# Products with zero-one matrices in fp32r, with a high and a low part

## The reference, cut to what matters

```python
cum = jnp.cumsum(log_f, axis=1).transpose(0, 2, 1)
...
logits = logits + cum[:, :, q0:kl, None] - cum[:, :, None, :kl]
...
p = jax.nn.softmax(jnp.where(mask, logits, NEG_INF), axis=-1)
```

```python
decay_in = jnp.exp(segsum(a))      # segsum[i, j] = sum of a[j+1..i] for i >= j, else -inf
cb = jnp.einsum('bclgn,bcsgn->bgcls', Cc, Bc)
y_diag = jnp.einsum('bgcls,bgrcls,bcsgrp->bclgrp', cb, decay_in, x_dt)
```

## Time and profile before

| | us |
|---|---|
| median of 3 runs (1515.44 to 1515.95) | 1515.65 |
| the profiled execution | 1515.26 |
| its span | 1513.5 |
| TensorE busy | 1435.5 |
| VectorE busy | 1060.0 |
| ScalarE busy | 757.6 |
| GpSimd busy | 70.2 |

### The profile page before, as it was taken

The page is one execution under the profiler, slowest core; times in us unless marked ns, Lnnn a source line. Parts: engine busy times, 40 slices in busy tenths (PEclk is TensorE's granted clock), DMA queues, the critical chain, the costliest instruction groups (busy, mean ns, idle before and its releaser), DMA issues.

```text
span 1513.5 us, 26922 instructions
## 1 busy us (share of the span) xinstructions
PE 1435.5 (95%) x9273; PEld 1293.6 (85%) x9273; DVE 1060.0 (70%) x1981; ACT 757.6 (50%) x1211; POOL 70.2 (5%) x87
## 2 busy tenths in 40 slices
PE   7889889999899997989989999999999999999997
PEld 7867769899798886889979999999999999988886
DVE  6897665555668577569997999555555555567775
ACT  6644654444556533454544555444444444444453
POOL 0200100000000621000000000000000000000000
PEclk9999999999999999999999999999999999999999
DMA  7442325565344522454546888755757566577753
GB/s 280 139 130 96 126 84 188 186 192 183 112 144 161 169 82 70 153 181 154 167 152 185 256 257 259 226 189 184 249 183 245 182 220 210 190 239 249 249 194 140
DMA packets 103208, 274.54 MB, mean 181 GB/s; under 512 B 8160, under 2 KB 41056, under 8 KB 102640
## 3 DMA queue, kind: packets, MB, share of 16 engines
q1 hardware_dynamic: 64832, 237.11, 48.4%
q10 hardware_dynamic: 38032, 34.63, 6.8%
q0 software_dynamic: 288, 2.10, 0.4%
HBM read 254.93 MB, written 18.87 MB: 181 GB/s over the span
## 4 chain that ended last, share of the span: by engine, by line
PE 80%; DVE 15%; ACT 2%; issue 2%; POOL 0%; DMA 0%; POOLq 0%; ACTq 0%; DVEq 0%; SPq 0%
PE Y L1803 43%; PE AO L1803 34%; DVE wl L950 4%; DVE CV L1034 2%; PE M L1803 2%; ACT wh L471 1%; DVE eqs L1558 1%; DVE I L1478 1%; DVE SCO L1494 1%; DVE I L1492 1%; DVE PU L1533 0%; DVE V L1500 0%; DVE V L1486 0%; DVE eqs L1572 0%; DVE xn L973 0%
## 5 line engine op out<-in xcount | busy, mean ns | idle before, releaser
L950 DVE TENSOR_TENSOR wl<-raw,wh 128x1024 fp32r<-128x1024 f32 x440 | 541.6, 1234 | 278.2 <-ACT wh L471 277.4
L471 ACT CAST wh<-raw 128x1024 fp32r<-128x1024 f32 x440 | 460.0, 1048 | 186.7 <-PE AO L1803 92.3
L1803 PE MATMUL AO<-xh,wh 128*128 128x256 f32 (+1 forms) x1776 | 511.0, 288 | 8.6 <-DVE wl L950 7.3
L1803 PE MATMUL AO<-xh,wl 128*128 128x256 f32 (+1 forms) x1776 | 503.4, 283 | 0.0
L1803 PE MATMUL AO<-xl,wh 128*128 128x256 f32 (+1 forms) x1776 | 503.4, 283 | 0.0
L1803 PEld LDWEIGHTS AO<-xh,wh 128*128 128x128 f32 x1776 | 338.5, 191 | 16.3 <-DVE wl L950 9.0
L1803 PEld LDWEIGHTS AO<-xl,wh 128*128 128x128 f32 x1776 | 337.8, 190 | 4.6 <-issue 0.2
L1803 PEld LDWEIGHTS AO<-xh,wl 128*128 128x128 f32 x1776 | 338.7, 191 | 0.0
L1803 PE MATMUL Y<-wh,peer_ah 128*128 128x512 f32 x512 | 200.7, 392 | 2.1 <-DVE peer_al L1620 2.1
L1803 PE MATMUL Y<-wh,peer_al 128*128 128x512 f32 x512 | 200.3, 391 | 0.0
L1803 PE MATMUL Y<-wl,peer_ah 128*128 128x512 f32 x512 | 199.1, 389 | 0.0
(11 more groups left out here) (305 smaller groups left out, 1672.2 us busy)
## 6 DMA issues: line engine op xcount, KB each, us to landing
raw<-in_stream SPq DMA_DIRECT2D x440, 512.0 KB, 3.4
gate_spill<-gstage ACTq DMA_DIRECT2D x32, 512.0 KB, 5.2
gates<-gate_spill ACTq DMA_DIRECT2D x6, 2048.0 KB, 14.9
gates<-gate_spill ACTq DMA_DIRECT2D x8, 512.0 KB, 7.2
rowg<-in_post SPq DMA_DIRECT2D x3, 512.0 KB, 4.4
X<-in_x SPq DMA_DIRECT2D x2, 512.0 KB, 4.8
memx<-in_mem SPq DMA_DIRECT2D x1, 1024.0 KB, 8.1
keys<-in_keys POOLq DMA_DIRECT2D x1, 1024.0 KB, 6.7
```

Source lines behind the costliest of these rows:

```text
L471: nc.scalar.copy(wh[:, s, :], raw[:, s, :]).then_inc(split_hi, 1)
L950: nc.vector.tensor_tensor(wl[:, s, :], raw[:, s, :], wh[:, s, :].bitcast(F32), ALU.subtract)\
L1803: return nc.tensor.matmul(o, a, b, start=start, stop=stop)
```

## The change

The operands of the products with zero-one matrices become fp32r. As fp32r holds fewer bits than float32, the other operand is split: a high part (the value rounded to fp32r) and a low part (the rest), each multiplied by the same zero-one matrix into the same accumulation.

- VectorE: two more steps after the forget logarithms (a copy to fp32r and a subtraction, tile logs) and two more after dt_a (tile da), each waiting for the one before.
- GpSimd: DEC is made twice (DEC and DECL), six products in place of three, the second three behind an added wait for norm_turned 4, as DECL lies where xn was; AU is made twice per k (AU and AUL), two products in place of one. A wait for da_split is added ahead of the scan's work.
- TensorE: logits and seg use fp32r products, twice as many for the decays and the segment sums; the mask product stays single, with 2 to the 100 in place of 1e30, a number that fp32r holds.
- The waits for DEC count to 6, those for AU to 2k + 2.

The products of queries and keys, of MM and XDT, of the states, of ac (line 2091 and on) and the turns stay plain float32.

```diff
@@ -36,6 +36,7 @@
 NEG = -1e30
+MASKED = 2.0 ** 100
 SLOTS = 4
@@ -150,11 +151,13 @@
         xl = sb("xl", [P, KT, TM], F32R)
-        ident = sb("ident", [P, P])
+        ident_r = sb("ident", [P, P], F32R)
+        ident = ident_r[:, :].bitcast(F32)
         masks_at = (nc.sbuf_base + 31) // 32 * 32
-        upper = sb("upper", [P, P])
-        later = sb("later", [P, P])
-        ones = sb("ones", [P, P])
+        upper_r = sb("upper", [P, P], F32R)
+        later_r = sb("later", [P, P], F32R)
+        ones_r = sb("ones", [P, P], F32R)
+        upper, later, ones = (t[:, :].bitcast(F32) for t in (upper_r, later_r, ones_r))
         neg_half = sb("neg_half", [P, 1])
@@ -173,7 +176,7 @@
         rowg = at("rowg", [P, 3, D], 8768)
-        mask = at("mask", [P, P], 21056)
+        mask = at("mask", [P, P], 21056, F32R)
         memx = at("memx", [P, TT, D], 22080)
@@ -186,7 +189,8 @@
         MV = at("MV", [P, TT, 512], 100384)
-        DEC = at("DEC", [P, FOX_H, 3, P], 104480)
+        DEC = (at("DEC", [P, FOX_H, 3, P], 104480, F32R), at("DECL", [P, FOX_H, 3, P], 63520, F32R))
+        logs = at("logs", [P, 2, 16], 59424 + 64, F32R)
         att_p = at("att_p", [P, 2, 512], 116768)
@@ -215,7 +219,8 @@
         CBM = at("CBM", [P, 4, P], 98336)
-        AU = at("AU", [P, 2, 3, P], 124192)
+        AU = (at("AU", [P, 2, 3, P], 124192, F32R), at("AUL", [P, 2, 3, P], 0, F32R, base=choice_at))
+        da = at("da", [P, 2, 2 * SSD_H], 78048, F32R)
         EE = at("EE", [P, 2, 3, P], 127264)
@@ -294,6 +299,7 @@
         cb_prod, cb_mask, ac_prod, ac_exp = sem("cb_prod"), sem("cb_mask"), sem("ac_prod"), sem("ac_exp")
+        da_split = sem("da_split")
         xdd_w, xdd_done, xdt_done, xd_done = sem("xdd_w"), sem("xdd_done"), sem("xdt_done"), sem("xd_done")
@@ -594,7 +600,7 @@
                     values_high(s - 2)
-                    act.wait_ge(dec_done, 3)
+                    act.wait_ge(dec_done, 6)
                     act.wait_ge(ln_xc, 1)
@@ -1069,6 +1075,12 @@
                     nc.vector.tensor_tensor(zf, z8, zf, ALU.subtract).then_inc(logf, 1)
+                    dve.wait_ge(logf, 1)
+                    z16 = SQ[:, 0, 0:16]
+                    nc.vector.tensor_copy(logs[:, 0, :], z16).then_inc(logf, 1)
+                    dve.wait_ge(logf, 2)
+                    nc.vector.tensor_tensor(logs[:, 1, :], z16, logs[:, 0, :].bitcast(F32), ALU.subtract)\
+                        .then_inc(logf, 1)
@@ -1257,6 +1269,11 @@
                     .then_inc(dt_a, 1)
+            dve.wait_ge(dt_a, 2)
+            nc.vector.tensor_copy(da[:, 0, :], dtz[:, 3, 24:72]).then_inc(da_split, 1)
+            dve.wait_ge(da_split, 1)
+            nc.vector.tensor_tensor(da[:, 1, :], dtz[:, 3, 24:72], da[:, 0, :].bitcast(F32), ALU.subtract)\
+                .then_inc(da_split, 1)
@@ -1673,21 +1690,21 @@
             nc.gpsimd.memset(ident[:, :], 0.0).then_inc(consts, 1)
-            nc.gpsimd.memset(mask[:, :], 0.0).then_inc(consts, 1)
+            nc.gpsimd.memset(mask[:, :].bitcast(F32), 0.0).then_inc(consts, 1)
             nc.gpsimd.memset(neg_half[:, :], -0.5).then_inc(consts, 1)
...
             pool.wait_ge(consts, 5)
-            nc.gpsimd.affine_select(out=ident[:, :], in_=ident[:, :], pattern=[[-1, P]], compare_op=ALU.not_equal,
+            nc.gpsimd.affine_select(out=ident_r[:, :], in_=ident[:, :], pattern=[[-1, P]], compare_op=ALU.not_equal,
                                     fill=1.0, base=0, channel_multiplier=1).then_inc(consts, 1)
-            nc.gpsimd.affine_select(out=upper[:, :], in_=ones[:, :], pattern=[[1, P]], compare_op=ALU.is_ge,
+            nc.gpsimd.affine_select(out=upper_r[:, :], in_=ones[:, :], pattern=[[1, P]], compare_op=ALU.is_ge,
                                     fill=0.0, base=0, channel_multiplier=-1).then_inc(consts, 1)
-            nc.gpsimd.affine_select(out=later[:, :], in_=ones[:, :], pattern=[[-1, P]], compare_op=ALU.is_gt,
+            nc.gpsimd.affine_select(out=later_r[:, :], in_=ones[:, :], pattern=[[-1, P]], compare_op=ALU.is_gt,
                                     fill=0.0, base=0, channel_multiplier=1).then_inc(consts, 1)
-            nc.gpsimd.affine_select(out=mask[:, :], in_=mask[:, :], pattern=[[-1, P]], compare_op=ALU.is_ge,
-                                    fill=-NEG, base=0, channel_multiplier=1).then_inc(consts, 1)
+            nc.gpsimd.affine_select(out=mask[:, :], in_=mask[:, :].bitcast(F32), pattern=[[-1, P]], compare_op=ALU.is_ge,
+                                    fill=MASKED, base=0, channel_multiplier=1).then_inc(consts, 1)
@@ -1716,11 +1733,14 @@
             pool.wait_ge(consts, 9)
-            pool.wait_ge(logf, 1)
-            zf = SQ[:, 0, 0:16].rearrange("p (j h) -> p j h", j=TT)
-            for n, (j, m) in enumerate(((0, later), (1, ones), (1, later))):
-                nc.gpsimd.tensor_tensor(DEC[:, :, n, :], zf[:, j, :][:, :, None].to_broadcast([P, FOX_H, P]),
-                                        m[:, None, :].to_broadcast([P, FOX_H, P]), ALU.mult).then_inc(dec_done, 1)
+            for part in range(2):
+                pool.wait_ge(logf, 2 + part)
+                if part:
+                    pool.wait_ge(norm_turned, 4)
+                z = logs[:, part, :].bitcast(F32).rearrange("p (j h) -> p j h", j=TT)
+                for n, (j, m) in enumerate(((0, later), (1, ones), (1, later))):
+                    nc.gpsimd.tensor_tensor(DEC[part][:, :, n, :], z[:, j, :][:, :, None].to_broadcast([P, FOX_H, P]),
+                                            m[:, None, :].to_broadcast([P, FOX_H, P]), ALU.mult).then_inc(dec_done, 1)
             for p in range(3):
@@ -1741,9 +1761,10 @@
                     pool.wait_ge(seg_prod, k - 1)
-                a = dtz[:, 3, 24 * (c + 1) + 3 * s:24 * (c + 1) + 3 * s + 3]
-                nc.gpsimd.tensor_tensor(AU[:, k % 2, :, :], a[:, :, None].to_broadcast([P, 3, P]),
-                                        upper[:, None, :].to_broadcast([P, 3, P]), ALU.mult).then_inc(au_done, 1)
+                for part in range(2):
+                    a = da[:, part, 24 * c + 3 * s:24 * c + 3 * s + 3].bitcast(F32)
+                    nc.gpsimd.tensor_tensor(AU[part][:, k % 2, :, :], a[:, :, None].to_broadcast([P, 3, P]),
+                                            upper[:, None, :].to_broadcast([P, 3, P]), ALU.mult).then_inc(au_done, 1)
@@ -1763,6 +1784,7 @@
             pool.wait_ge(xdd_w, 2)
+            pool.wait_ge(da_split, 2)
             pool.wait_ge(tr_out, 3)
@@ -1958,13 +1980,14 @@
                 if kind != "mem":
-                    d = DEC[:, :, :, :].rearrange("p (a e) n k -> p e a n k", e=2)[:, e, 2 * m:2 * m + n, :, :]
-                    if kind == "first":
-                        mm(o, upper[:, :], d[:, :, 0, :], True, False)
-                    else:
-                        mm(o, upper[:, :], d[:, :, 1:3, :].rearrange("p a n k -> p a (n k)"), True, False)
-                        mm(o[:, :, 0:P], ones[:, :], d[:, :, 0, :], False, False)
-                    mm(o[:, :, w - P:], ident[:, :], mask[:, None, :].to_broadcast([P, n, P]), False, False)
+                    for part in range(2):
+                        d = DEC[part][:, :, :, :].rearrange("p (a e) n k -> p e a n k", e=2)[:, e, 2 * m:2 * m + n, :, :]
+                        if kind == "first":
+                            mm(o, upper_r[:, :], d[:, :, 0, :], part == 0, False)
+                        else:
+                            mm(o, upper_r[:, :], d[:, :, 1:3, :].rearrange("p a n k -> p a (n k)"), part == 0, False)
+                            mm(o[:, :, 0:P], ones_r[:, :], d[:, :, 0, :], False, False)
+                    mm(o[:, :, w - P:], ident_r[:, :], mask[:, None, :].to_broadcast([P, n, P]), False, False)
                 for i, (h, j, w) in enumerate(members(g)):
@@ -1996,7 +2019,7 @@
             pe.wait_ge(norm_lo, 4)
-            pe.wait_ge(dec_done, 3)
+            pe.wait_ge(dec_done, 6)
             pe.wait_ge(a_free, A_BASE["qk"] + 8)
@@ -2169,11 +2192,13 @@
             def seg(k):
-                pe.wait_ge(au_done, k + 1)
+                pe.wait_ge(au_done, 2 * k + 2)
                 if k:
                     pe.wait_ge(seg_exp, k)
-                mm(AO[:, 0, 0:3 * P], later[:, :], AU[:, k % 2, :, :].rearrange("p a b -> p (a b)"),
-                   True, True).then_inc(seg_prod, 1)
+                for part in range(2):
+                    ins = mm(AO[:, 0, 0:3 * P], later_r[:, :], AU[part][:, k % 2, :, :].rearrange("p a b -> p (a b)"),
+                             part == 0, part == 1)
+                ins.then_inc(seg_prod, 1)
```

## The result

The changed kernel took **1521.82 us**, the median of 5 runs (1517.49 to 1522.54), against 1515.65 for the kernel before (1514.17 to 1515.95, 5 runs): a ratio of 1.0036, 95% interval 1.002 to 1.0051. Two later sets of runs gave +3.1 and +5.2 us. The profiled run is the fastest of the first five, 1517.49 us with a span of 1515.8, so its trace understates the difference.

What follows compares the result with a forecast made beforehand. TensorE carries 80% of the span, but VectorE bounds the forgetting attention. Terms 2.9 + 0.4 + 1.4 + 1.8 = +6.5 us on the profiled 1515.26, with 0.4 for the median, gave 1522.2 us; range 1515.0 to 1527.5.

Steps and rivals of the forecast that it cites:

- Three more DEC products: Forgetting attention: GpSimd's three added products hold up VectorE, +4.0 us, bounds 2.0 and 7.4.
- VectorE's waits for groups 4 and 5: Attention logits: faster TensorE removes VectorE's waits of 0.56 and 0.95 us, −1.5 us.
- Two steps after the forget logarithms: Attention: VectorE's added copy and subtraction, 0.2 us each, +0.4 us, bounds 0.1 and 0.8.
- Attention in sum: Forgetting attention, its three terms together: 4.0 + 0.4 − 1.5 = +2.9 us.
- Two steps after dt_a: Ahead of the xbc conv: VectorE's copy and subtraction, +0.4 us (0.1 to 0.8), all on the chain.
- First chunk: Scan: six AU pairs cost VectorE 3.3 us, less idle time and slack, +1.4 us, bounds −2.1 and +3.5.
- Second chunk: Scan: added AU products delay MM steps, two segment sums give back 0.6, +1.8 us, bounds −1.0 and +4.0.
- stages that I took as untouched: The rest of the kernel: fp32r constants, MASKED and moved tiles change no count or size, nothing added.
- the products win: Rival: GpSimd's added work costs nothing and TensorE's savings arrive, −3.8 us, 1511.8 us; chance 0.10.
- Half of it: Rival: attention costs as forecast but the scan absorbs its pairs (−1.0), +2.3 us, 1518.0 us; chance 0.17.
- It doesn't do what it says: Rival: fp32r products run at the plain pitch, so TensorE pays twice, about 1531 us; chance 0.03.
- The clock: Rival: longer pauses bring two or three more TensorE clock dips, adding 2.6 to 3.9 us, 1525.5 us; chance 0.15.

Runs made afterwards that it cites:

- e4: Kernel before with GpSimd making the three DEC products a second time into an unread tile, matmuls plain float32: 1519.9 us, ratio 1.0027.
- e3: Changed kernel with GpSimd making only the high DEC and AU, each multiplied twice by TensorE: 1512.22 us, ratio 0.9982 to the kernel before.
- e11: The changed kernel run a third time, nothing else altered: 1520.52 us against 1515.31 for the kernel before.
- e2: Kernel before with the scan part of the change alone (with the two steps after dt_a), attention as before: 1514.4 us, ratio 0.9993.
- e10: The scan part of the change alone on the kernel before, run again: 1514.76 us against 1515.31.
- e7: Whole change, but ScalarE makes both parts of DEC and the low part of AU: 1511.44 us, ratio 0.9974 to the kernel before.
- e12: Kernel before with only the copy and subtraction after dt_a added, results unread: 1511.56 us, ratio 0.9972.

## Why the prediction was right, and where it was not

The time was right to 0.4 us (1522.2 against 1521.8), but three sets of runs spread over 3 us, and the spans of the three traces are only 2.3, 3.1 and 4.4 us longer than before, as stages outside of the sum gave time back. So close a hit is luck; what held is the direction, and above all the cost of the DEC products. By the steps of the sum:

- **Three more DEC products, +4.0**: 3.94 in the rows, 3.95 in e4. The ml steps spared 0.9 us of the fourth product, as worked out. The upper bound for the fp32r type wasn't needed.
- **VectorE's waits for groups 4 and 5, −1.5**: both gone, and e3 has −1.3 for the stage, with the two small steps in it. One group's zero-one products took 0.99 us, not 0.82, and had taken 1.82, not 1.72; counted from the turns ahead of them the group saved 0.90, as I had it.
- **Two steps after the forget logarithms, +0.4**: starts at 62.83, 63.03, 63.24. Attention in sum +2.7, predicted +2.9.
- **Two steps after dt_a, +0.4**: +0.5 between the last dtz step and XDM, in each of the eight traces that have them. But I took all of it to reach the end. It doesn't: the next stage gives back 1.4, by the dip at 490 to 496 us. This step of the sum failed in its sign: with that dip it is −0.9, and the kernel with nothing but these steps is 3.75 us faster, the part beyond −0.9 unexplained.
- **First chunk, +1.4**: +0.4, the term mis-sized. I took 0.55 us for each pair, 3.3 in all; VectorE's busy time grew by 2.35 in the whole chunk, as the second products partly met steps that read PSUM (the ST step at 559.27 took 0.56) and VectorE's idle time. And "its shorter segment sums come to nothing" was too strict: with its waits between sums (1.65 at k = 2, 0.69 at k = 4), TensorE's 2.07 us less of work counted against 2.47 of waiting. MM for k = 4 came later than TensorE was ready, and so did k = 2, which I hadn't named; at k = 7, the other that I named, it was late by 0.1 us only.
- **Second chunk, +1.8**: +2.2, with the same clock (0.89) before and after. Late are a split (1.84 at 571.49), a YO sum (1.31) and an SP step (1.06), as the lock has it.

The terms sum to +5.8 us where I had +6.5. The stages that I took as untouched moved as well: by +0.6 to −1.3 between the conv and dt_a, by −1.4 behind XDM, and by −2.3 or +0.5 at the end, depending on the run. The third trace of the change (e11) shows the slow end of this: windows of the first trace, then of e11:

```profile
780.00:790.00 10.00, 7.70 (x60) 7.30 (x61) 9.93 (x15) 5.40 (x8) 0.00 (x0) 1.00 0.34 112
810.00:820.00 10.00, 7.45 (x64) 7.28 (x63) 8.96 (x21) 4.10 (x7) 0.00 (x0) 1.00 0.38 129
```

```profile
780.00:790.00 10.00, 7.57 (x51) 7.49 (x51) 9.93 (x13) 4.03 (x6) 0.00 (x0) 0.83 0.33 105
810.00:820.00 10.00, 7.44 (x53) 7.27 (x52) 8.38 (x21) 4.10 (x7) 0.00 (x0) 0.85 0.34 119
```

The same kernel, two dips more, 2.8 us more from the last gate to the end. The Trainium skill, "TensorE: Matmul & The Clock Gate", section "Part 1: The HAM clock gate (the "warmup" mystery)", says that the point at which the clock first rises can differ between runs of one kernel. These two traces show such a difference in the middle of a kernel: 1.00 in one and 0.83 in the other at 780 to 790 us.

Of the rivals, "the products win" fell with e4. "Half of it" had the scan at −1.0 and fell with its +0.4 and +2.1 in the change, e2 and e10, though the +3.1 of the second set of runs alone would not have ruled it out. "It doesn't do what it says" fell with the pitches: 0.12 us for 256 columns, 0.18 for 384. "The clock" was half right. It expected longer pauses to bring dips at the scan; there are as many as before. New ones came in the attention (0.76 at 98 to 112 us, before 1.00), where VectorE sets the end and the stage came out as summed. What it missed is that dips also vanish, and that their balance differs from kernel to kernel by what may be several microseconds.

## What to carry to other kernels

Before TensorE work is bought with GpSimd work, read what VectorE does at that time: each DEC product on GpSimd cost a VectorE that was on the chain up to four fifths of its own length (1.64 of 2.07 us), and the same values made by ScalarE between its casts cost nothing. Read a small change by the lengths between marks that both traces have; the whole time carries the clock's dips too, and two unread steps moved it by 3.75 us. And run the halves of a change: their sum needn't be the whole.

## What the runs showed of the hardware

- With a dead half microsecond added (0.19 and 0.21 us on VectorE), a dip of TensorE's clock 57 us later is gone, in all of eight traces with it (three of the change, e2, e10, e3, e7, e12) and in none of six without. I expected the clock to be noise on top of the sum.
- A kernel has its own level of mean clock: e2 and e10 both 0.984, the change 0.978 to 0.979 three times. The level alone doesn't order the kernels: e3 at 0.978 is 3.3 us faster than the kernel before at 0.981.
- GpSimd writes fp32r at the speed of float32 (2.07 us for 128x1024, 0.83 for 128x384).
- A first fp32r product behind plain ones starts the next only after 0.31 us (124.52 to 124.83) where 0.23 was the pitch. In this group that cost nothing in sum: the first starts sooner behind the plain ones (0.36 us behind the turns at 124.16, where a plain product started 0.43 behind those at 113.87).
